# Linear attention in a fused two-block kernel: states on quarters of the TensorE array, outputs of two heads on row halves, in four pieces

## What is computed

```
def gla_chunk_causal(q, k, v, log_alpha):
    ...
    bcum = jnp.cumsum(la, axis=2)
    b_end = bcum[:, :, -1:]
    k_dec = k * jnp.exp(b_end - bcum)
    q_dec = q * jnp.exp(b_end)
    ...
    updates = jnp.einsum("bnthd,bnthv->bnhdv", k_dec, v)
    decay = jnp.exp(b_end[:, :, 0])
    def step(state, inp):
        d, upd = inp
        return d[..., None] * state + upd, state
    ...
```

## Time and profile before

| | us |
|---|---|
| runs, median of 3 | 2465.02 |
| lowest, highest | 2460.68, 2466.03 |
| span of the profiled execution | 2457.9 |
| PE busy in it | 2368.7 (96%) |
| DVE, ACT, POOL busy | 1412.9, 1138.7, 894.2 |

### The profile page before, as it was taken

The page is one execution under the profiler, slowest core; times in us unless marked ns, Lnnn a source line. Parts: engine busy times, 40 slices in busy tenths (PEclk is TensorE's granted clock), DMA queues, the critical chain, the costliest instruction groups (busy, mean ns, idle before and its releaser), DMA issues.

```text
span 2457.9 us, 31373 instructions
## 1 busy us (share of the span) xinstructions
PE 2368.7 (96%) x12074; PEld 1954.5 (80%) x12074; DVE 1412.9 (57%) x1963; ACT 1138.7 (46%) x1778; POOL 894.2 (36%) x665
## 2 busy tenths in 40 slices
PE   5999999989999999999999999999999999999998
PEld 5778788868888888876678877788878888888887
DVE  6255499958885330139963753332576666666665
ACT  5322388868884221249952474231333333333334
POOL 1111234236652112335521222112255555555651
PEclk8999999999999999999999999999999999999999
DMA  7244300000003131100031311013111111111121
GB/s 301 75 129 145 94 6 1 1 19 1 1 1 112 59 108 43 52 1 1 10 112 38 121 44 43 18 35 120 43 52 52 52 52 52 52 52 52 52 60 69
DMA packets 152487, 143.21 MB, mean 58 GB/s; under 512 B 10358, under 2 KB 140692, under 8 KB 150420
## 3 DMA queue, kind: packets, MB, share of 16 engines
q1 hardware_dynamic: 152340, 141.22, 18.0%
HBM read 124.43 MB, written 16.78 MB: 57 GB/s over the span
## 4 chain that ended last, share of the span: by engine, by line
PE 81%; ACT 8%; issue 5%; DVE 4%; POOL 1%; DMA 1%; SPq 0%; ACTq 0%; DVEq 0%; POOLq 0%
PE ps L260 38%; PE ps L2608 14%; PE ps L2625 9%; PE ps L1103 4%; PE ps L1126 3%; PE ps L1113 3%; ACT C_PR L1773 1%; ACT B_PR L1186 1%; ACT B_PTH L1180 1%; PE ps L2584 1%; PE ps L1662 1%; ACT C_PTH L1781 1%; PE ps L2052 1%; PE ps L2064 1%; PE ps L1641 1%
## 5 line engine op out<-in xcount | busy, mean ns | idle before, releaser
L249 POOL TENSOR_TENSOR WL<-WR,WH 128x1024 fp32r<-128x1024 f32 (+1 forms) x89 | 207.5, 2332 | 827.3 <-ACT WH L244 827.2
L260 PE MATMUL ps<-HH,WH 128*128 128x512 f32 (+1 forms) x1136 | 362.3, 400 | 0.0
L260 PE MATMUL ps<-HL,WH 128*128 128x512 f32 (+1 forms) x1136 | 353.4, 392 | 0.0
L260 PE MATMUL ps<-HH,WL 128*128 128x512 f32 (+1 forms) x1136 | 352.7, 392 | 0.0
L260 PEld LDWEIGHTS ps<-HL,WH 128*128 128x128 f32 (+1 forms) x1136 | 213.9, 188 | 47.3
L260 PEld LDWEIGHTS ps<-HH,WL 128*128 128x128 f32 (+1 forms) x1136 | 213.9, 188 | 47.1
L260 PEld LDWEIGHTS ps<-HH,WH 128*128 128x128 f32 (+1 forms) x1136 | 210.0, 189 | 51.8 <-issue 10.1
L2838 DVE TENSOR_TENSOR XF<-ps,XF 128x1024 f32<-128x1024 f32 x168 | 201.5, 1220 | 32.4 <-PE ps L2625 25.8
L2608 PE MATMUL ps<-HC,WSH 128*128 128x512 f32 x640 | 197.0, 389 | 0.0
L1139 DVE TENSOR_REDUCE NM<-ps 128x1 f32<-128x1024 f32 x128 | 156.0, 1220 | 35.0 <-PE ps L1103 34.1
L2525 POOL TENSOR_TENSOR WSL<-WSR,WSH 128x512 fp32r<-128x512 f32 x100 | 131.0, 1310 | 107.6 <-ACT WSH L2519 107.6
(11 more groups left out here) (433 smaller groups left out, 5227.2 us busy)
## 6 DMA issues: line engine op xcount, KB each, us to landing
WS<-in_w_ffn_in SPq DMA_DIRECT2D x44, 512.0 KB, 5.0
MKW<-in_ada_w SPq DMA_DIRECT2D x32, 512.0 KB, 4.1
spill<-X SPq DMA_DIRECT2D x3, 4096.0 KB, 13.6
OW<-in_w_ffn_out SPq DMA_DIRECT2D x22, 512.0 KB, 3.4
WR<-in_w_in SPq DMA_DIRECT2D x20, 512.0 KB, 3.6
WR<-in_odd_w_in SPq DMA_DIRECT2D x19, 512.0 KB, 3.7
WR<-in_even_w_in SPq DMA_DIRECT2D x17, 512.0 KB, 4.8
AWK<-in_ada_w SPq DMA_DIRECT2D x8, 1024.0 KB, 9.4
```

The lines of the kernel that those rows point to most:

```text
L249: pool.tensor_tensor(low[:, :, :], raw[:, :, :], high[:, :, :].bitcast(F32), ALU.subtract).then_inc(*w_low.up(t))
L260: last = pe.matmul(ps[0:w.m, 2 * s + h, :], wt[:, k, :], x[:, k, halves(h)], start=(k == 0 and n == 0), stop=(k == w.kt - 1 and n == 2))
```

## The change

`pe_states(p)` takes the place of `pe_state(c)`. It does two chunks (2p and 2p + 1) behind every second feature, so it is called 8 times where `pe_state` was called 16 times. Each matmul has 64 contraction rows (the chunk's tokens: even chunks below, odd ones above), 64 weight columns (one head's keys), and 128 value columns, and writes 64 partitions of PSUM: a quarter of the array, and only the block that is used. A pair of chunks has 8 such matmuls, in the order chunk, head for each f. It waits for the states of both chunks of the pair before it. The two heads of an f now lie in one bank, one below the other, so that `dve_state` does both in one instruction of 128 partitions.

`pe_outputs(f, part)` takes the place of `pe_output(hd)`: the two heads of f in turn, chunk by chunk, four chunks in each of four pieces. The pieces stand at (14, 4) to (14, 7) and (17, 0) to (17, 3). The sums of heads 2 and 3 move from (17, 6) and (17, 7) to (18, 0) and (18, 1).

```diff
-    def pe_state(c):
-        r = rows(c % 2, CHUNK)
+    def pe_states(p):
+
         for f in range(2):
-            if c >= 2:
-                pe.wait_ge(*state.at(c - 2, f))
-            else:
-                pe.wait_ge(*v_copied.at(3))
-            pe.matmul(ps[:, 4 + 2 * (c % 2) + f, 0:2 * P], KDT[r, f, c // 2, :], VT[r, c // 2, f * 2 * P:(f + 1) * 2 * P],
-                      start=True, stop=True).then_inc(*state_mm.up(c, f))
-
-    def pe_output(hd):
-        f, hr = hd // 2, rows(hd % 2, HD)
-        if hd < 2:
+            for e in range(2):
+                if p:
+                    pe.wait_ge(*state.at(2 * (p - 1) + e, f))
+                else:
+                    pe.wait_ge(*v_copied.at(3))
+            for e in range(2):
+                r = rows(e, CHUNK)
+                for h in range(2):
+                    last = pe.matmul(ps[rows(h, HD), 4 + 2 * e + f, 0:P], KDT[r, f, p, rows(h, HD)],
+                                     VT[r, p, rows(2 * f + h)], start=True, stop=True)
+                last.then_inc(*state_mm.up(2 * p + e, f))
+
+    def pe_outputs(f, part):
+
+        if part == 0 and f == 0:
             pe.wait_ge(*state.at(NCH - 1, 1))
             pe.wait_ge(*ev_act.at(S_QRY[1]))
-        else:
-            pe.wait_ge(*o_done.at(hd - 2))
-        for c in range(NCH):
+        elif part == 0:
+            for h in range(2):
+                pe.wait_ge(*o_done.at(h))
+        for c in range(4 * part, 4 * part + 4):
             cs = rows(c, CHUNK)
-            last = pe.matmul(pair(4 + 2 * (hd % 2))[:, cs], SS[hr, f, c, :], QG[hr, f, cs], start=True, stop=True)
-        last.then_inc(*o_mm.up(hd))
+            for h in range(2):
+                hr = rows(h, HD)
+                last = pe.matmul(pair(4 + 2 * h)[:, cs], SS[hr, f, c, :], QG[hr, f, cs], start=True, stop=True)
+                if c == NCH - 1:
+                    last.then_inc(*o_mm.up(2 * f + h))
...
             elif 12 <= j <= 14 and 0 <= 8 * (j - 12) + k - 4 < NCH:
-                pe_state(8 * (j - 12) + k - 4)
-            elif (j, k) in ((14, 5), (14, 7), (17, 0), (17, 1)):
-                pe_output({(14, 5): 0, (14, 7): 1, (17, 0): 2, (17, 1): 3}[j, k])
-            elif (j, k) in ((15, 4), (15, 5), (17, 6), (17, 7)):
-                pe_output_sums({(15, 4): 0, (15, 5): 1, (17, 6): 2, (17, 7): 3}[j, k])
+                if k % 2 == 0:
+                    pe_states((8 * (j - 12) + k - 4) // 2)
+            elif j == 14 and k >= 4:
+                pe_outputs(0, k - 4)
+            elif j == 17 and k < 4:
+                pe_outputs(1, k)
+            elif (j, k) in ((15, 4), (15, 5), (18, 0), (18, 1)):
+                pe_output_sums({(15, 4): 0, (15, 5): 1, (18, 0): 2, (18, 1): 3}[j, k])
...
     def dve_state(c):
         for f in range(2):
+            bank = 4 + 2 * (c % 2) + f
             dve.wait_ge(*state_mm.at(c, f))
             if c:
                 dve.wait_ge(*state.at(c - 1, f))
-            for h in range(2):
-                hr, bank = rows(h, HD), 4 + 2 * (c % 2) + f
-                if c:
-                    last = dve.scalar_tensor_tensor(SS[hr, f, c, :], SS[hr, f, c - 1, :], DEC[hr, f, c:c + 1],
-                                                    ps[hr, bank, rows(h)], ALU.mult, ALU.add)
-                else:
-                    last = dve.tensor_copy(SS[hr, f, c, :], ps[hr, bank, rows(h)])
-            last.then_inc(*state.up(c, f))
+                dve.scalar_tensor_tensor(SS[:, f, c, :], SS[:, f, c - 1, :], DEC[:, f, c:c + 1], ps[:, bank, 0:P], ALU.mult,
+                                         ALU.add).then_inc(*state.up(c, f))
+            else:
+                dve.tensor_copy(SS[:, f, c, :], ps[:, bank, 0:P]).then_inc(*state.up(c, f))
```

## The result

The changed kernel takes 2435.66 us (median of 4 runs, 2434.37 to 2435.99), against 2465.53 us for the kernel before on the same chip (4 runs, 2460.68 to 2468.97): a ratio of 0.9886 with a 95% interval of 0.9872 to 0.9900, by the ratio 28 us less. The forecast was 2446.4 with a range from 2440.5 to 2459.5.

A forecast was written before the change was run, and what follows sets the result against it. PE's own stream was taken to bound the kernel. States 10.8, wait 2.8, clock 1.7 and outputs 10.5 replace 44.4 us, gaining 18.6 from the 2457.9 span; plus 7.1 gives 2446.4 us, range 2440.5 to 2459.5.

The forecast's parts named there:

- What bounds it: Whole kernel: PE holds 81% of the chain, and what leaves its stream moves the end unless a wait replaces it.
- Part 1: States on quarters: a pair of chunks costs 0.42 us fixed plus 0.93 streaming, 1.35; 8 pairs 10.8 us, before 20.7.
- Rival 1: States: quarters of the same rows do not overlap, 1.40 us streaming a pair instead of 0.93; 2449.7 us, chance 0.15.
- Part 2: Last pair (chunks 14, 15): PE waits 2.8 us for DVE's state steps, then half clock costs 1.7 us.
- Part 3: Outputs in pieces: 8 pieces at 1.31 us, 10.5 us instead of 23.7, and the lowered clock goes.
- Part 4: Moved sums and the spread at (18, 5): no wait, priced at nothing, at most 1 us if the spread's cover fails.
- Rival 2: States and outputs: nothing overlaps, 17.2 us each, a gain of only 6.3 us; 2458.7 us, chance 0.18.
- rival 3: States through outputs: the clock drops to half in every packed stretch, 52 us lost, slower at 2498 us; chance 0.05.
- Span to median: Whole kernel: the median of the runs was taken to stand 7.1 us above the profiled span, 2439.3 giving 2446.4.

The follow-up runs named there:

- The kernel without the pause: Changed kernel with DVE's gate product and low part for tile 13 moved behind the state steps of chunks 12 to 15: 2432.53 us, then 2433.01 us.
- 23.8 in the second: Changed kernel run again without edit beside more runs of the kernel before: 2438.69 us against 2462.44, ratio 0.9906.
- the halves: Kernel before with only the states changed, 2448.25 us, and with only the outputs changed, 2448.63 us; ratio 0.9953 each.
- the second profiles: Profiles of the kernel before run again without edit, 2459.71 us, and of the changed kernel run again without edit, 2438.69 us.

## Why the prediction was right and wrong

Two terms failed, and between them they are 10.0 of the 10.7 us by which the forecast was too high: the way from the span to the median (5.8) and the size of a pair (4.2). With the first put right the time lies inside the range, moved down by as much; with the second alone it does not.

- *What bounds it.* Right: the chain stayed with PE, and what left its stream moved the end. The rest of the program behind the region took 815.4 us before and 815.2 after.
- *Part 1, the size of a pair.* Wrong, and the step of the mechanism that failed: "What overlaps is then a matmul's second record with the next matmul's first: 8 matmuls at one record's distance each". The fixed 0.4 us was right; the streaming was 4 rounds and not 8, since the first records of all four quarters start before the second record of any. 0.82 instead of 1.35, 4.2 us over 8 pairs. The rows of two row halves could not tell the two apart: each matmul there is one record. With two halves both models ask for the same number of rounds, which is why the outputs came out right (1.27 against 1.31).
- *Rival 1.* Wrong: one chunk on quarters showed column halves side by side.
- *Part 2, the pause.* Right: 3.0 us at the forecast place, on DVE's state steps, behind the low part LM. That 2.8 came so near has some luck in it, since two smaller misses work against each other: PE came to the wait 0.5 us earlier, with the shorter pair, and DVE's three steps and the way to PE took 0.99 (1546.28 to 1547.27) instead of 1.18. The clock drop behind it cost 1.6 us in the first profile (1.7 forecast), and came in four of the five profiles with the same pause. The kernel without the pause confirmed the cause.
- *Part 3, outputs.* Right in size. The clock stayed at 1.00, but of the reason given ("A piece is shorter and does more") the first half was not needed: one long run of both heads keeps the clock as well.
- *Part 4.* Right: the sums and spreads follow their features without a wait.
- *Rival 2 and rival 3.* Neither came: pairs and pieces overlap, and the clock is at 1.00 in both output stretches.
- *Span to median.* Wrong, and the larger of the two: "the median of the runs stands 7.1 above the span". That was the distance of one execution from three other ones. A run stands 1.3 above its own span, and the other 5.8 us belonged to the runs of before in that comparison, three of which were longer than any later run of that kernel; the changed kernel's executions do not owe it. Why they were long stays open. With 1.3 the forecast would have been 2440.6, and with the pair at 0.82 as well 2436.4.
- *How much it really gains.* 28 us in the first comparison, 23.8 in the second, 24.3 from the halves. The traces' regions give 23.0, and 21.3 for the second profiles, which come from two chips. For the halves, measured on one chip, the medians give 1.8 and 2.7 us more than the regions of one execution each; that is left open.

## What to carry to other kernels

When small float32 matmuls are laid on quarters of the array, count the rounds of the fullest quarter and not the instructions: here 8 matmuls on four quarters cost what 4 on two cost, and the fixed 0.4 us for entering and leaving the shape was as much as all the streaming, so it pays to put as many quarters as possible into one insertion. Doing two chunks at a time also asks for the step of two chunks to be ready; look at what stands ahead of that step on the other engine, since one move of two instructions there was worth another 5.7 us by the medians, and 3.1 to 4.6 by the regions. And hold a span against the time of the same execution, not against the median of other ones.

## What the runs showed of the hardware

- Records of float32 matmuls do not start in the order of the kernel's source across tiles of the array: the first records of four quarters start within 0.02 us, then, 0.109 us apart, the later ones. With 8 matmuls on four quarters the order in the source was worth 0.02 us; with 8 matmuls on two halves, four and four, 0.5 us. A tile's first record passed three waiting records of another tile and not seven. Whether PE alone makes this order, or the translation of the source has a part in it, no run here shows.
- Two column halves of the same rows load and stream together (8 records in 0.82 us with the switches).
- Runs of 3.7 us with one head (32 records on one row half) were followed or met by half clock in 9 of the 12 such runs in three profiles (the two of before, and the states alone). Runs of the same length with two heads (64 records on both halves) were in none of 4, and pieces in none.
- The same pause of PE, 3.0 us, was followed by 3.4 us of half clock in three executions, by 6.8 in one and by none in one.
